# Linear attention beside a matrix product: the next tile's cumulative gate and keys in a step of their own

## The reference

```
logg = log_sigmoid(gr @ w_alpha + b_alpha) / 16
b  = cumsum(logg) within a chunk;  b_last = its last row
qt = q * exp(b);  kt = k * exp(-b);  kd = k * exp(b_last - b)
att = tril(qt @ kt.T);  o = att @ v + qt @ s
s  = exp(b_last) * s + kd.T @ v          (the next chunk's state)
```

## Time and profile before

| | us |
|---|---|
| median of 3 runs | 2421.78 (2416.04 to 2422.0) |
| profiled execution | 2420.89 |
| its span | 2419.2, granted TensorE clock 0.982 |
| TensorE busy | 2286.2 (95%) |
| VectorE busy | 1739.0 (72%) |
| ScalarE busy | 1002.5 (41%) |
| GpSimd busy | 1206.2 (50%) |

### The profile page before, as it was taken

How to read it: one execution, slowest core, us unless ns; L and a number is a source line. 1 busy time by engine, 2 the same in 40 slices (tenths; PEclk the granted TensorE clock), 3 DMA queues, 4 the chain that set the end, 5 groups by cost and what they waited for, 6 DMA issues and landing times. The chain is left out here.

```text
span 2419.2 us, 39403 instructions
## 1 busy us (share of the span) xinstructions
PE 2286.2 (95%) x12602; PEld 2085.4 (86%) x12602; DVE 1739.0 (72%) x2584; ACT 1002.5 (41%) x1957; POOL 1206.2 (50%) x1251
## 2 busy tenths in 40 slices
PE   7998889999899998899999999999999988999997
PEld 6898768988679876799999998899999987999996
DVE  6576766276573666688988988767667677878886
ACT  5444353343244435344444445433333335444443
POOL 3653533214314234778778785444444445455552
PEclk9999999999999999899999999999999999999999
DMA  3543535544347563744444447644454456555553
GB/s 121 195 162 123 183 113 193 178 120 152 113 169 247 155 225 132 260 174 147 165 173 148 160 176 258 207 160 146 140 161 151 139 183 231 199 187 191 188 194 107
DMA packets 264595, 412.72 MB, mean 171 GB/s; under 512 B 14108, under 2 KB 186993, under 8 KB 264497
## 3 DMA queue, kind: packets, MB, share of 16 engines
q1 hardware_dynamic: 264497, 411.45, 50.6%
HBM read 313.24 MB, written 98.16 MB: 170 GB/s over the span
## 5 line engine op out<-in xcount | busy, mean ns | idle before, releaser
L1571 PE MATMUL ps<-xo,wq 128*128 128x384 f32 (+1 forms) x1848 | 600.1, 325 | 22.1 <-POOL wq L979 5.9
L1572 PE MATMUL ps<-xo,wq 128*128 128x384 f32 (+1 forms) x1848 | 599.4, 324 | 0.0
L1573 PE MATMUL ps<-xo,wq 128*128 128x384 f32 (+1 forms) x1848 | 599.3, 324 | 0.0
L2365 DVE TENSOR_TENSOR resid<-resid,ps 128x512 f32<-128x512 f32 (+1 forms) x728 | 477.3, 680 | 76.2 <-PE ps L1573 45.6
L979 POOL TENSOR_TENSOR wq<-wu_raw,wq 128x256 fp32r<-128x256 f32 x396 | 378.5, 979 | 111.7 <-ACT wq L1091 111.7
L1571 PEld LDWEIGHTS ps<-xo,wq 128*128 128x128 f32 x1848 | 350.8, 190 | 45.2 <-issue 18.8
L1572 PEld LDWEIGHTS ps<-xo,wq 128*128 128x128 f32 x1848 | 351.4, 190 | 20.2
L1573 PEld LDWEIGHTS ps<-xo,wq 128*128 128x128 f32 x1848 | 351.9, 190 | 0.0
L2382 DVE SCALAR_TENSOR_TENSOR up_y<-up_u,params,up_y 128x768 f32<-128x768 f32 (+1 forms) x264 | 287.5, 1089 | 50.1 <-ACT up_y L1135 31.4
L498 POOL TENSOR_TENSOR wq<-wu_raw,wq 128x256 fp32r<-128x256 f32 x174 | 147.3, 869 | 302.5 <-ACT wq L1212 302.5
L1571 PE MATMUL ps<-wd_hi,hid_hi 128*128 128x512 f32 x704 | 277.2, 394 | 11.1 <-DVE resid L2365 11.0
(11 more groups left out here) (246 smaller groups left out, 4289.6 us busy)
## 6 DMA issues: line engine op xcount, KB each, us to landing
wq<-w_ops SPq DMA_DIRECT2D x176, 512.0 KB, 4.5
wu_raw<-in_w_up_dram SPq DMA_DIRECT2D x89, 512.0 KB, 4.2
w_ops<-wq SPq DMA_DIRECT2D x88, 512.0 KB, 2.6
wq<-m_ops SPq DMA_DIRECT2D x80, 512.0 KB, 4.0
wd_raw<-in_w_down_dram SPq DMA_DIRECT2D x66, 512.0 KB, 5.2
wu_raw<-in_w_in_dram SPq DMA_DIRECT2D x40, 512.0 KB, 5.1
m_ops<-wq SPq DMA_DIRECT2D x40, 512.0 KB, 3.3
x_in<-in_x_prompt_dram SPq DMA_DIRECT2D x32, 512.0 KB, 4.7
```

What stands on the lines that cost most here:

```text
L1571: pe.matmul(out, lh, rh, start=(first and n == 0), stop=False, skip_group_check=skip)
L1572: pe.matmul(out, ll, rh, start=False, stop=False, skip_group_check=skip)
L1573: last = pe.matmul(out, lh, rl, start=False, stop=end, skip_group_check=skip)
L2365: last = dve.tensor_tensor(resid[0:m, t, s], resid[0:m, t, s], ps[0:m, bank, :], ALU.add)
```

## The change

A new step U stands between X and Y (in tiles that have a Y and a next tile). TensorE makes the next tile's `gate_sums` there, ScalarE b_cum and k_exp (`gate_exps`), VectorE the distances and the keys' multiply (`key_decays`). Behind Y ScalarE makes k_end's exp, the square of the output, and then, behind the second state, the exps of queries and decay, from b_cum in place of PSUM (`query_exps`); VectorE, behind `next_state(t, 1)`, multiplies k_end and then the queries (`query_decays`). 31 products are now dealt out over 23 steps (18 in block 2). Behind X, U, Y, Z of tiles 0 to 4 in blocks 0 and 1 they are 1 1 2 1, 1 2 1 1, 2 1 1 2, 1 1 2 1, 1 2 1 1; tile 2 has 6.1 6.2 behind X, 6.3 behind U, 6.4 behind Y, 6.5 6.6 behind Z. In block 2, tiles 0 to 3: 1 2 2 1, 2 2 2 1, 2 2 1 2, 2 2 1 2.

```diff
         def mix_events(b):
-            steps = [(s, t) for t in range(TILES[b]) for s in ("XYZ" if tile_cols(b, t)[1] == P else "XZ")]
+            steps = [(s, t) for t in range(TILES[b]) for s in ("XUYZ" if tile_cols(b, t)[1] == P else "XZ")
+                     if s != "U" or t + 1 < TILES[b]]
@@ ScalarE, gate_exps(t) @@
                     mix.wait(act, "cum", t + 1)
+                    mix.wait(act, "q_exped", t)
                     mix.wait(act, "dist", t)
+                    mix.wait(act, "att_done", t)
                     act.activation(b_cum[:, :, 0:m], b_ps[:, :, 0:m], ACT.Copy)
-                    act.activation(q_exp[0:HK, :, 0, 0:m], b_ps[0:HK, :, 0:m], ACT.Exp, scale=1 / TAU)
-                    act.activation(q_exp[HK:P, :, 1, 0:m], b_ps[HK:P, :, 0:m], ACT.Exp, scale=1 / TAU)
+                    mix.inc(act.activation(k_exp[:, :, 0:m], b_ps[:, :, 0:m], ACT.Exp, scale=-1 / TAU), "cum_read")
+
+                def query_exps(t):
+                    m = tile_cols(b, t)[1]
+                    mix.wait(act, "cum_read", t + 1)
                     mix.wait(act, "state0", t)
                     mix.wait(act, "state1", min(t, BTS[b] // P))
-                    act.activation(decay[:, :, 0:m // CHUNK], b_ps[:, :, CHUNK - 1:m:CHUNK], ACT.Exp, scale=1 / TAU)
-                    mix.inc(act.activation(k_exp[:, :, 0:m], b_ps[:, :, 0:m], ACT.Exp, scale=-1 / TAU), "cum_read")
+                    act.activation(q_exp[0:HK, :, 0, 0:m], b_cum[0:HK, :, 0:m], ACT.Exp, scale=1 / TAU)
+                    act.activation(decay[:, :, 0:m // CHUNK], b_cum[:, :, CHUNK - 1:m:CHUNK], ACT.Exp, scale=1 / TAU)
+                    mix.inc(act.activation(q_exp[HK:P, :, 1, 0:m], b_cum[HK:P, :, 0:m], ACT.Exp, scale=1 / TAU), "q_exped")
@@ ScalarE, the steps @@
+                    if ev[0] == "U":
+                        gate_exps(t + 1)
                     if ev[0] == "Y":
+                        if more:
+                            k_end_exp(t + 1)
                         o_square(t)
-                    if ev[0] == ("Y" if tile_cols(b, t)[1] == P else "X") and more:
-                        gate_exps(t + 1)
-                        k_end_exp(t + 1)
+                        if more:
+                            query_exps(t + 1)
@@ TensorE, the steps @@
+                    if ev[0] == "U":
+                        gate_sums(t + 1)
                     if ev[0] == "Y":
                         outputs_2(t)
-                        if more:
-                            gate_sums(t + 1)
@@ VectorE @@
-                def decays(t):
+                def key_decays(t):
                     mix.wait(dve, "cum_read", t + 1)
+                    mix.wait(dve, "turned", t)
...
                     mix.inc(last, "dist")
+                    dve.tensor_tensor(k_exp[:, :, 0:m], k_exp[:, :, 0:m], qk[:, 2:4, c0:c0 + m], ALU.mult)
+
+                def query_decays(t):
+                    mix.wait(dve, "k_end_exp", t + 1)
+                    dve.tensor_tensor(k_end[:, :, 0:m], k_end[:, :, 0:m], qk[:, 2:4, c0:c0 + m], ALU.mult)
+                    mix.wait(dve, "q_exped", t + 1)
                     for e in range(2):
                         r = slice(e * HK, (e + 1) * HK)
-                        dve.scalar_tensor_tensor(q_exp[r, :, e, 0:m], q_exp[r, :, e, 0:m], HK ** -0.5, qk[r, 0:2, c0:c0 + m],
-                             ALU.mult, ALU.mult)
-                    dve.tensor_tensor(k_exp[:, :, 0:m], k_exp[:, :, 0:m], qk[:, 2:4, c0:c0 + m], ALU.mult)
-                    mix.wait(dve, "k_end_exp", t + 1)
-                    mix.inc(dve.tensor_tensor(k_end[:, :, 0:m], k_end[:, :, 0:m], qk[:, 2:4, c0:c0 + m], ALU.mult), "qk_exp")
+                        last = dve.scalar_tensor_tensor(q_exp[r, :, e, 0:m], q_exp[r, :, e, 0:m], HK ** -0.5, qk[r, 0:2, c0:c0 + m],
+                             ALU.mult, ALU.mult)
+                    mix.inc(last, "qk_exp")
...
+                    if ev[0] == "U":
+                        key_decays(t + 1)
                     if ev[0] == "Y":
                         next_state(t, 1)
                         if more:
-                            decays(t + 1)
+                            query_decays(t + 1)
```

More of the change, by code:

```diff
@@ L385, in mix_counts @@
                 "u_done": 2, "y_first": CJ, "conv_step": 2 * CJ, "y_done": 2, "pre": nt, "pre_b": nt,
-                "soft": 3 * nt, "lg": nt, "cum": nt, "cum_read": nt, "dist": nt, "k_end_exp": nt, "qk_exp": nt,
+                "soft": 3 * nt, "lg": nt, "cum": nt, "cum_read": nt, "dist": nt, "k_end_exp": nt, "q_exped": nt, "qk_exp": nt,
                 "att_done": nt, "att_read": nt, "turned": nt, "turned_read": nt, "d1": nt, "d2": full,
@@ L1377, in _ @@
                         gate_exps(0)
+                        query_exps(0)
                     if ev[0] == "C":
@@ L1701, in scores @@
                     m = tile_cols(b, t)[1]
+                    mix.wait(pe, "cum_read", t + 1)
                     mix.wait(pe, "qk_exp", t + 1)
@@ L2100, in decays @@
                     mix.inc(last, "dist")
+                    dve.tensor_tensor(k_exp[:, :, 0:m], k_exp[:, :, 0:m], qk[:, 2:4, c0:c0 + m], ALU.mult)
+                def query_decays(t):
+                    c0, m = tile_cols(b, t)
+                    mix.wait(dve, "k_end_exp", t + 1)
+                    dve.tensor_tensor(k_end[:, :, 0:m], k_end[:, :, 0:m], qk[:, 2:4, c0:c0 + m], ALU.mult)
+                    mix.wait(dve, "q_exped", t + 1)
                     for e in range(2):
                         r = slice(e * HK, (e + 1) * HK)
-                        dve.scalar_tensor_tensor(q_exp[r, :, e, 0:m], q_exp[r, :, e, 0:m], HK ** -0.5, qk[r, 0:2, c0:c0 + m],
-                                                 ALU.mult, ALU.mult)
-                    dve.tensor_tensor(k_exp[:, :, 0:m], k_exp[:, :, 0:m], qk[:, 2:4, c0:c0 + m], ALU.mult)
-                    mix.wait(dve, "k_end_exp", t + 1)
-                    mix.inc(dve.tensor_tensor(k_end[:, :, 0:m], k_end[:, :, 0:m], qk[:, 2:4, c0:c0 + m], ALU.mult), "qk_exp")
+                        last = dve.scalar_tensor_tensor(q_exp[r, :, e, 0:m], q_exp[r, :, e, 0:m], HK ** -0.5, qk[r, 0:2, c0:c0 + m],
+                                                        ALU.mult, ALU.mult)
+                    mix.inc(last, "qk_exp")
                 def masked_scores(t):
@@ L2241, in pair_event @@
                         mix.wait(dve, "c12_read", 4)
-                        decays(0)
+                        key_decays(0)
+                        query_decays(0)
                 for ev in mix_events(b):
```

## The result

The median is 2432.71 us (2432.39 to 2434.77, 5 runs) against 2416.08 for the kernel before in the same runs (2414.25 to 2422.0): +16.6 us between the two medians. The ratio over all these runs is 1.0063, 15 us, with a 95% interval of 1.0049 to 1.0077. The two profiled executions, from which the rows are read, took 2432.62 and 2420.89 us, +11.7.

What follows compares the result with a forecast made beforehand. TensorE, busy 95% of the span, was taken as the bound. From 2420.9 us, idle +18.2 (sums 12.0, scores 15.7, gla_y 7.0, against 16.5), clock 0, about 1 given back: 2438 us; overall range 2419 to 2449.

Steps and rivals of the forecast that it cites:

- case A: Whole kernel: the summed waits come as drawn; 2438 us, 2431 to 2446; chance 0.65.
- Edit 1: Sums moved from behind Y to U: TensorE waits there for the log gate, 12.0 us against 2.4 before.
- Edit 2: Behind Y: keys' part leaves the chain to the scores; wait 0.8 us with one product, none with two.
- Edit 3: Before the scores: Y slides behind one more product, whose VectorE work delays the state update; 15.7 us against 11.2.
- Edit 4: Fewer products from Z to X: X waits for gla_y, 7.0 us in all against 2.9 before.
- Edit 5: The new waits between engines cost 0; bound +1 us if a weight copy behind U comes late.
- Clock: Half-clock stretches behind TensorE's long waits, three before and four after: taken as equal, 0, bounds -3 and +3.4 us.
- Rival C: Short waits drop the clock: nine new waits each bring a half-clock stretch costing 1.7 us; 2453 us; chance 0.09.
- The sum: TensorE idle 34.7 us against 16.5, +18.2; clock 0; about 1 us given back; 2438 us.
- Rival B: VectorE's products do not delay the state update, no wait over 2 us; 2418 us, or 2412; chance 0.14.
- D: Waits only move: what U adds is taken from later ones, idle stays at 16.8 us; 2421 us; chance 0.12.
- my line at 2.3 us: TensorE's clock: half clock seen only behind waits of 2.3 us and more, not with 1.4 and 1.1 close together.

Runs made afterwards that it cites:

- after_short_gate: After with only the first of the log gate's three ScalarE functions made (Exp and Ln left out); 2423.50 us, ratio 1.0018 to the kernel before.
- deal_only: The kernel before, operations in their old steps, with the new deal of products (U an empty step); 2430.12 us, ratio 1.0046.
- split_no_u: After's parted keys and queries at before's steps and deal, no U, sums behind Y; 2414.66 us, ratio 0.9983 to before.
- u_late_keys: After at the old deal, U directly ahead of Y, VectorE's keys' part behind the second state update, ScalarE's square ahead of k_end's exp; 2421.90 us.
- after_no_tap: After with VectorE's two taps behind product 6.3 working on 2 columns instead of the whole row; 2430.42 us, ratio 1.0048 to before.

## Why the prediction was right

2438 was forecast, +17 on an execution of 2420.9, with 2431 to 2446 for case A. 2432.71 was measured: inside, near the lower edge. The +16.6 between the medians looks closer to +17 than the forecast was, since the median of before was 2416.08 in these runs, 4.8 under the execution that I had started from. The ratio gives +15, the two profiled executions +11.7. The mechanism came as drawn, with waits before the sums and a scores' wait in tile 2 that grew; the sizes of its terms were less good. Step by step:

- **Edit 1, the wait at U:** nine waits, 10.0 us, forecast nine and 12.0. A one-product gap with VectorE free waits 0.84, not 1.1: the product's last matmul ends 2.3 us behind the gate product (484.39 and 482.08 in block 1's first round), and I took 2.07. Block 0's first wait is 2.2, forecast 1.9; in this execution VectorE's weight sums also waited 0.5 us there for the raw weights. after_short_gate shows the cause.
- **Edit 2, the shorter chain behind Y:** right in kind. At the same deal it takes 8.1 us off the scores (deal_only against after). That it is not only VectorE catching up while TensorE waits at U is borne out by after_short_gate, where most of those waits are gone and the scores' do not grow (11.8). split_no_u shows a small gain. Where VectorE was free the wait is 0.59 (tile 4, blocks 0 and 1), forecast 0.8.
- **Edit 3, Y behind one more product:** tile 2, 3.7 and 3.2 us, forecast 3.7 twice; state update at +13.1, forecast +13.6; scores at +16.6, forecast +17.1. Block 0's tile 1 waits 1.9 and not 2.9, with 0.7 before the mean squares, which the sum did not have (ScalarE's square stood behind weight copies that waited for VectorE's weight sums). The scores together 13.2, forecast 15.7. That the taps are a part is shown (1.6 us of the wait); that they are all of the lengthening is not.
- **Edit 4, one product between Z and X:** forecast 7.0, measured 4.0 from the traces' gaps (0.1 to 0.2 each where 0.2 to 0.3 was taken; block 0's 1.0 did not come, probably since TensorE ran at half clock while VectorE caught up; block 2's 2.2 did, forecast 2.4). The most mis-sized term, and the one sign of mine that failed: the wait on gla_y was to double, and went from 2.9 to 3.3.
- **Edit 5, the new waits:** no wait in the trace of after is put down to them.
- **Clock:** taken as 0 between bounds of -3 and +3.4; it was +1.7. Rival C as priced, a half-clock stretch behind each of the nine waits at U, is refuted for this kernel: none of the nine, 0.8 to 2.2 us, has one behind it, and the mixers hold three as before. A part of it stands: one of the three, at 173 us, came behind two short waits close together (0.7 and 1.9). What the Trainium skill, "TensorE: Matmul & The Clock Gate", section "A second HAM failure mode: psum-queue depth-cycling", says of very short idle times between groups of matmuls, that they make the clock swing when they are frequent, did not come with the waits at U, which lie 8 us or more from the next wait.
- **The sum:** idle +11.0 instead of +18.2 (27.9 against 16.8 us in the three stretches; by kind of wait 27.2 against 16.5), clock +1.7. From X of tile 0 to Z of the last tile the three blocks take 112.3 + 107.4 + 80.8 = 300.5 us against 108.2 + 100.7 + 74.8 = 283.7, and block 2 has one product (1.6) more in it: +15.2. So 2.5 us are in neither sum: in block 1 a one-wait round of 5 products takes 0.17 us more than before's once its waits are taken off (17.79 - 0.95 against 17.07 - 0.40), and after has 28 idle gaps in the mixers where before has 15. That they are in restarting the weight loads is argued, not shown. The rest of the span, where the change does nothing, took 3.5 us less in after's profiled execution than in before's, where I had taken 1; 2.9 of it lie between the mixers of blocks 1 and 2 (207.5 us against 210.4), and why is not known. So the total came out right partly by luck: the waits were forecast 7 us too long, the 2.5 and 1.7 us were left out, and the base and the rest of the span are within the scatter of single executions.

Rival B (the split as drawn) fails at its own point, the state update within 1 us of Y's end: it starts 2.6 us behind it. D (waits only move) fails: they grew. The idle time of 27.9 us is clear of the 22 under which I had called the prediction wrong.

What no step of mine said is that the two halves of the change do not add: the deal alone costs 11 us, U at the old deal 11 us, both together about 15 (0.63%). U at the old deal puts the keys' part ahead of the state update with nothing between them, which u_late_keys bears out. That with products between U and Y VectorE gets there in time, and pays instead in the gaps, is my reading of the two sums of waits; no run tests it by itself.

## What to carry to other kernels

A step that is cut in two does not only move its instructions; where filler work is dealt out by step, it re-deals all of it, and each gap must be held against the longest chain that has to pass in it (here 3.1 us of log gate against 2.3 us with one product in it). On an in-order engine, work made early stands ahead of something: ask what, and who waits for that. Try the deal alone first: it is a change of a line, and here all four kernels that beat the one before kept the old steps.

## What the hardware showed that I had not expected

The length of a wait did not settle the clock. In after a half-clock stretch came at 173 us, behind waits of 0.7 and 1.9 us with 1 us between them, and behind the two of 3.2 and 3.7; but u_late_keys had waits of 2.85 and 2.82 us before the scores and kept its clock, as the windows around them show, where before lost it behind 2.3 and 2.7:

```profile
186.00:200.00 14.00, 11.15 (x69) 9.90 (x69) 13.06 (x29) 4.56 (x10) 2.48 (x4) 1.00 0.10 39
525.00:538.00 13.00, 10.18 (x63) 8.93 (x63) 11.28 (x27) 3.94 (x9) 1.43 (x2) 1.00 0.26 81
```

The same wait in the same place can go either way. Block 2's third X waited 2.19 us for gla_y both in after and in after_no_tap, with a wait of 0.54 some 5 us ahead of it in both; after kept its clock, and after_no_tap lost 1.7 us of it:

```profile
826.00:838.00 12.00, 9.27 (x65) 7.91 (x64) 9.52 (x20) 3.92 (x9) 2.33 (x3) 1.00 0.36 111
821.00:833.00 12.00, 9.27 (x54) 8.29 (x54) 8.14 (x20) 2.53 (x5) 1.96 (x2) 0.86 0.36 111
```

So my line at 2.3 us held for before only, and a few us of these kernels' differences, and of their scatter, may be the clock's.

The median of the kernel before moved between sets of runs (2416.1, 2419.5, 2419.9, 2418.9), by a quarter of this change.
